# Moving one gate panel's filling from one attention branch's slots to the next

## The reference, cut to what matters

```
gated = jnp.concatenate([ya * jax.nn.silu(ag), yb * jax.nn.silu(bg),
                         yc * jax.nn.silu(cg), ym * jax.nn.silu(mg)], axis=-1)
y = gated @ w_out
return _layer_norm(alpha * x + y, ln_gain, ln_bias)
```

## Time and profile before

| what | us |
|---|---|
| median of three runs | 3514.69 |
| the profiled execution's own time | 3516.74 |
| its span in the trace | 3514.9 |
| TensorE busy in it | 3358.1 (96%) |
| mean granted TensorE clock | 0.99 of full |

### The profile page before, as it was taken

One profiled execution on the slowest core, in us unless ns is written; L12 is line 12 of the kernel. 1 busy time (PEld: TensorE's weight loads), 2 busy tenths in 40 slices (PEclk: granted clock), 3 DMA queues, 4 the chain that ended last, 5 costly groups with the idle time before them and its releaser, 6 DMA issues.

```text
span 3514.9 us, 48538 instructions
## 1 busy us (share of the span) xinstructions
PE 3358.1 (96%) x19500; PEld 1697.3 (48%) x19500; DVE 1515.2 (43%) x2327; ACT 959.1 (27%) x1742; POOL 1509.7 (43%) x986
## 2 busy tenths in 40 slices
PE   7999997999999799999997999999999989999999
PEld 4555653645554344444443445555545434444444
DVE  4364557145546733333114355555555653333100
ACT  1434422234332410000001455545454321000000
POOL 3555651444664233333331555455555423333332
PEclk9999999999999999999998999999999999999999
DMA  3122112112121011111112111111112111111112
GB/s 126 39 50 59 57 54 92 43 49 62 36 78 38 30 54 48 54 48 51 50 49 110 34 50 53 50 50 42 42 50 90 52 36 51 51 48 54 50 50 81
DMA packets 55196, 194.27 MB, mean 55 GB/s; under 512 B 7408, under 2 KB 7792, under 8 KB 54512
## 3 DMA queue, kind: packets, MB, share of 16 engines
q1 hardware_dynamic: 53728, 187.15, 17.0%
q10 hardware_dynamic: 1296, 4.72, 0.4%
HBM read 172.97 MB, written 12.58 MB: 53 GB/s over the span
## 4 chain that ended last, share of the span: by engine, by line
PE 88%; DVE 4%; issue 3%; ACT 2%; POOL 1%; DMA 0%; SPq 0%; DVEq 0%; POOLq 0%; ACTq 0%
PE pair L1049 26%; PE pair L1051 25%; PE pair L1050 25%; PE pair L1252 3%; PE pair L1221 2%; PE pair L1233 2%; PE pair L1426 1%; PE pair L1452 1%; PE pair L1437 1%; DVE arena L1880 1%; POOL panel_parts L860 1%; PE pair L1380 1%; DVE residual L1880 1%; PE pair L1069 1%; PE pair L1210 0%
## 5 line engine op out<-in xcount | busy, mean ns | idle before, releaser
L1049 PE MATMUL pair<-operand,panel_parts 128*128 128x512 f16 x2816 | 1075.9, 382 | 77.5 <-POOL panel_parts L860 43.8
L1050 PE MATMUL pair<-operand,panel_parts 128*128 128x512 bf16 x2816 | 1073.4, 381 | 0.0
L1051 PE MATMUL pair<-operand,panel_parts 128*128 128x512 f16 x2816 | 1073.0, 381 | 0.0
L859 POOL TENSOR_SCALAR panel_parts<-panel_raw 128x1024 f16<-128x1024 f32 (+3 forms) x286 | 296.1, 1035 | 1541.2 <-PE pair L1051 1029.6
L860 POOL TENSOR_TENSOR panel_parts<-panel_raw,panel_parts 128x1024 bf16<-128x1024 f32 (+3 forms) x286 | 633.0, 2213 | 23.9
L1049 PEld LDWEIGHTS pair<-operand,panel_parts 128*128 128x128 f16 x2816 | 276.3, 98 | 436.1 <-issue 138.4
L1049 PE MATMUL pair<-arena,panel_parts 128*128 128x512 f16 (+2 forms) x1200 | 453.2, 378 | 10.1 <-DVE arena L1880 3.1
L1051 PE MATMUL pair<-arena,panel_parts 128*128 128x512 f16 (+2 forms) x1200 | 452.0, 377 | 0.0
L1050 PE MATMUL pair<-arena,panel_parts 128*128 128x512 bf16 (+2 forms) x1200 | 452.0, 377 | 0.0
L893 POOL TENSOR_SCALAR arena<-arena,row_inv 128x256 f32<-128x256 f32 (+7 forms) x256 | 339.4, 1338 | 255.7 <-DVE row_inv L1946 255.7
L1051 PEld LDWEIGHTS pair<-operand,panel_parts 128*128 128x128 bf16 x2816 | 276.6, 98 | 336.2 <-issue 6.6
(11 more groups left out here) (191 smaller groups left out, 3853.3 us busy)
## 6 DMA issues: line engine op xcount, KB each, us to landing
panel_raw<-in_wgu SPq DMA_DIRECT2D x88, 512.0 KB, 3.5
panel_raw<-in_wl SPq DMA_DIRECT2D x58, 512.0 KB, 3.6
panel_raw<-in_wm SPq DMA_DIRECT2D x56, 512.0 KB, 3.6
panel_raw<-in_wdn SPq DMA_DIRECT2D x32, 512.0 KB, 3.5
residual_spill<-residual SPq DMA_DIRECT2D x16, 512.0 KB, 3.9
residual<-residual_spill SPq DMA_DIRECT2D x15, 512.0 KB, 6.2
panel_raw<-in_wl SPq DMA_DIRECT2D x18, 384.0 KB, 3.1
panel_raw<-in_wdn SPq DMA_DIRECT2D x16, 384.0 KB, 3.1
```

What stands on the lines that cost most here:

```text
L859: chained(nc.gpsimd.tensor_scalar(hi[:, 0:cols], RAW[:, s, 0:cols], HI_MAX, -HI_MAX, ALU.min, ALU.max))
L1049: nc.tensor.matmul(out, stat[0], mov[0], start=first, stop=False)
L1050: nc.tensor.matmul(out, stat[0], mov[1], start=False, stop=False)
L1051: return nc.tensor.matmul(out, stat[1], mov[0], start=False, stop=last)
```

## The change

mg1 leaves the end of b's list and opens m's. The order of all panels, their loads and their pieces is what it was; what changes is which part of which slot each step stands in.

```diff
     "c": ["ur", "un0.0", "cg1.0", "un0.1", "un1", "cg1.1", "uk0", "uk1.0", "mq0.0", "uk1.1", "uv0", "uv1", "mq0.1", "mq1", "bg0"],
-    "b": ["bg1", "mk0", "mk1", "mv0", "mv1", "mg0", "mg1"],
-    "m": [f"o{n}" for n in range(8)],
+    "b": ["bg1", "mk0", "mk1", "mv0", "mv1", "mg0"],
+    "m": ["mg1"] + [f"o{n}" for n in range(8)],
 }
...
                 layer_panels(l, "b")
+                layer_panel(l, "mg1")
 
                 sp.wait_ge(slot_scores, SCORES_AT[first_slot(l, "b") + TT - 1, 1])
```

## The result

The kernel after takes **3534.96 us** (median of five runs, 3527.59 to 3538.77), the kernel before 3514.69 in five runs beside them (3513.36 to 3518.15). The ratio is 1.0054, 95% interval 1.0040 to 1.0068: slower by 19 us (20 by the two medians), where 7.7 were forecast. The sign was right. The size was not, and 3535 lies above the range of 3511 to 3531. One execution of the experiment all_three, 3% longer than the others at a lower granted clock, is left out of all comparisons.

A forecast was written before the change was run, and what follows sets the result against it. TensorE was taken as the bound (busy 96%), with slack in b and almost none in m. Per layer +5.4 + 0.3 + 1.8 − 5.1 = +2.4; 3514.7 + 4.8 + 2.9 (clock) = 3522.4 us, range 3511 to 3531.

The forecast's parts named there:

- m's growth, +5.4 a layer: Slots 41 to 46: two more steps each, less small waits, take the six from 67.53 to 72.9 us.
- the clock's +2.9: Both layers: clock falls after new waits in slot 30 (2.25) and before p0 (2.4) add 2.9 us.
- b, −5.1 forecast: Stage b: shortened by 5.1 us a layer of 10.4 removed, as chains on other engines hold many slots.
- Slot 40, +0.3 forecast: Slot 40: gets one step and loses a short wait, +0.3 us a layer.
- The end of the layer, +1.8 forecast: Layer end: centring behind o7's last addition delays p0's split and the first output tile, +1.8 us a layer.
- I take half: Clock: no falls give 4.8 us in total, all four 10.6; half the fall cost, 2.9, was taken.
- p0's fall, priced at 1.2: Before p0's first product: a clock fall costs 1.2 us, not 1.7, as part lies in the wait.
- a wait of 1.54 leaves the clock alone: Slot 39: its 1.54 us wait left the clock at 1.00, while waits above 2 were followed by falls.
- all four would fall: Clock: by the throttled default alone, falls follow all four new waits, result 3525.3 us.
- rival 2: Stage b gives nothing back and the price is m's alone, 15 us, 3529.7; chance 0.20.
- rival 1: Stage b gives back all 10.4 us a layer: 3509, or 3505.4 with p0's split hidden; chance 0.14.
- rival 3: POOL isn't late: slot 30 gains 2.0 us, the layer's end loses nothing, 3511.4; chance 0.11.

The follow-up runs named there:

- all_three: Changed kernel with centring packed to end sooner, POOL's splits in b held to part 3, and b's empty part moved to part 3: 3524.52 us (1.0020).
- before_again: The kernel before, unchanged, run for a second trace: 3517.67 us, one run.
- filled_early: Changed kernel with useless TensorE transposes in the waits of slots 30, 39 (writing the free bank) and before p0's first product: 3528.69 us (1.0030).
- split_held: Changed kernel with POOL's panel splits of b's parts 0, 1 and 2 held to part 3 of the same slot: 3529.28 us (1.0041).
- after_again: The changed kernel, unchanged, run for a second trace: 3533.83 us, one run.

## Why the prediction was wrong

Two terms of the sum failed: m's growth, +5.4 a layer, was reckoned from a slot of 11.3 that is one of two lengths of that slot, and the clock's +2.9 left out slot 39's wait, priced that of p0 too low and took waits of 1.54 for harmless. The paths and waits were in the main those described.

Point by point, per layer but for the clock, with before_again and filled_early as the pair without falls at the new waits.

- **b, −5.1 forecast, −4.45 measured.** Slots 24, 25 to 29, 32 to 34, 36 to 38 are each within 0.11 of their term, and DVE's chain in slots 25 to 27 and 33 held: no gain. The place of the loss in POOL's stream was right (slot 30: wait 1.87, length −0.05 for +0.28). The miss is slot 35, 0.2 for 0.7. It is ACT's chain again, as in slots 28 and 36: the second transposes wait for ACT's copy of the first group, which stands behind an exponent. mg1's split, which POOL does in this slot of the changed kernel, is not the reason: in split_held it comes after slot 35's second head is scaled (at 1006.58), and the wait, 0.29, and the slot, 6.98, are the same. The first row is of the changed kernel, the others of split_held:

```profile
1016.34 0.74 PE L1234 MATMUL pair<-ident,arena 128*128 128x128 f32 x5 [0.29 <-ACT stats L1537]
...
1004.69 1.89 POOL L894 TENSOR_SCALAR arena<-arena,row_inv 128x640 f32<-128x640 f32 x1 [0.31 <-DVE row_inv L1951]
...
1008.18 0.74 PE L1238 MATMUL pair<-ident,arena 128*128 128x128 f32 x5 [0.29 <-ACT stats L1541]
```

- **m's six slots, +5.4 forecast, +7.5 measured.** This is the step of the work that failed: "a slot goes from 11.3 to about 12.14". It goes to 12.24. I added the steps to 11.31 less its 0.45 of idle; but 0.32 of that idle is one that a slot has or doesn't have. The forecast for the slot was near (0.1 off), the base was not: from 10.99, two steps cost 1.25. Against the first trace's own 67.53 the growth is 5.9; against the mean of the twelve layers traced of the kernel before and its variants, 66.4, it is about 7. How long these slots are in the executions without a trace, on which the median rests, stays open. mg1's gate end cost nothing, as argued: slot 41 is 12.24, like the rest.
- **Slot 40, +0.3 forecast, +0.36 measured.**
- **The end of the layer, +1.8 forecast, +2.2 measured.** From slot 46's values to the second half of the first output tile it is 22.28 in filled_early (1138.14 less 1115.86) for 20.10, and the stretch to the end of the wait of 2.9 grows by the same 2.2 in both layers. The order of events is the one described: o7's additions, centring, split.
- **Sum:** −4.45 + 7.5 + 0.36 + 2.2 = +5.6 a layer (about 5.1 with m against the mean of 66.4), 11.2 for both, where +2.4 and 4.8 were forecast. filled_early, with no fall at the new waits, stands 11.9 above the kernel before.
- **The clock, +2.9 forecast for both layers, +6.3 measured.** "I take half" was not the fault: a fall followed 14 of the 26 such waits that stand unfilled in the traces, though four of six in each of the changed kernel's own two. The fault is that slot 39 was priced at nothing, although its part 0 became idle: three waits a layer and not two. A step taken from a slot that can't shorten is a longer wait. The text even says so of slots 25 to 27 ("the idle before them grown by 0.65"; as shown, TensorE's idle there grew by 0.41, 0.23 and 0.31) and does not carry it to slot 39. The second fault is p0's fall, priced at 1.2, which costs 1.8. And the reading that a wait of 1.54 leaves the clock alone was wrong in the trace of the kernel before itself. The fall near 844, which I put behind a wait above 2, stands behind one of 1.54, in slot 17:

```profile
844.46 0.39 PE L1049 MATMUL pair<-arena,panel_parts 128*128 128x512 f16 x1 [1.54 <-DVE arena L1883]
...
844.00:848.00 4.00, 3.54 (x22) 1.99 (x22) 1.47 (x6) 1.87 (x4) 2.63 (x3) 0.71 0.00 0
```

That wait of slot 17 is followed by a fall in 21 of the 32 layers traced, slot 39's of the same 1.54 in none of 16. Why the two places differ, no run tells. The prediction's step that by the default state alone "all four would fall" was not borne out either: slot 30's two in after_again did not. Why slot 30's wait and slot 39's took turns in the changed kernel's two traces is not shown; that sparing slot 30 brings the fall to slot 39 is not so in split_held, where neither has one.

The traces allow a count of their own. The second trace of the changed kernel is 16.2 longer than that of the kernel before: slots 41 to 46 +15.0, slots 24 to 40 −5.1 (two falls in it), from slot 46 to the second layer's slot 23 +4.2, from the second slot 46 to the end +2.2, the start −0.1. By the first traces it is 18.2, by the two medians 20.3 and by the ratio 19. The sum above gives 11.2 and 6.3, 17.5. What is left is within the 10 us by which runs of one kernel spread. The clock also falls in code that neither kernel changes, at 41.6 in one trace and not in another of the same kernel, and this part stays open.

The rivals: rival 2 (b gives nothing) gave 3529.7, the nearest number, by luck: its reason is refuted by the slots; rival 1 and rival 3 fell with slots 25 to 27 and with the wait of slot 30.

## What to carry to other kernels

Work taken from a stage shortens only the parts of it that this engine's own work fills; everywhere else it turns into idle time, and a longer idle time can cost the clock of what follows. A wait that one trace shows without a fall is not harmless by that: look for the same length elsewhere and in a second trace. Price each slot twice, once for its length and once for the length of its waits. And take the base of a stage from more than one execution: a slot that repeats can have one of two lengths, here 0.32 apart.

## What was not expected of the hardware

- Two overlapping operations of DVE and POOL that start within 0.011 us of each other share out their delay in one of two ways: addition 1.01 and scalings 3.62, or 0.69 and 4.18. A lead of 0.002 us for the addition is enough for the second, in all 60 overlaps traced. Which way it goes can change from slot to slot or hold for a whole layer.
- Equal waits of 1.87 (slot 30) and 2.14 (slot 39) lead to a fall of the granted clock in one trace and not in the next, and so does one of 1.54 (slot 17, 21 of 32). Useless transposes for 1.47 us in these waits and 1.91 us in p0's kept the clock at its higher level in all 12 waits that they filled, and gave back 6.3 us by medians.
